# Low parts of every second weight block in two stages: from VectorE's subtraction to a transfer that adds in place

## The reference

```python
    y = h.astype(u.dtype) * jax.nn.silu(gate)
    return y @ w_out                                        # a_w_out
...
        h = h + _rmsnorm(y, norm_post[i])
        h = h + jax.nn.sigmoid(h @ ple_w_gate[i]) * (p[i] @ ple_w_proj[i])
```

## Time and profile before

| | |
|---|---|
| median of 3 runs | 2148.67 us (2148.39 to 2149.68) |
| span of the profiled execution | 2146.7 us; the median is 2.0 us above it |
| PE busy | 2101.1 us, 98% of the span |
| DVE busy | 1592.8 us, 74% |
| ACT busy | 1026.9 us, 48% |
| POOL busy | 99.5 us, 5% |
| DMA queue of SP | 445.78 MB, 61.1% of 16 engines |
| low parts by DVE | 636, 774.6 us |
| high parts by ACT | 636, 671.6 us |
| aout / the 12 single tiles of pleg | about 284.4 to 378.6 us / 428 to 496 us of the span |

### The profile page before, as it was taken

How to read it: one execution, slowest core, us unless ns; L and a number is a source line. 1 busy time by engine, 2 the same in 40 slices (tenths; PEclk the granted TensorE clock), 3 DMA queues, 4 the chain that set the end, 5 groups by cost and what they waited for, 6 DMA issues and landing times.

```text
span 2146.7 us, 31802 instructions
## 1 busy us (share of the span) xinstructions
PE 2101.1 (98%) x12800; PEld 1830.9 (85%) x12800; DVE 1592.8 (74%) x2357; ACT 1026.9 (48%) x1560; POOL 99.5 (5%) x81
## 2 busy tenths in 40 slices
PE   7999999999999999999999999999999999999997
PEld 7787799787888888899999888878888888888886
DVE  7778699698889777667877898576766766656655
ACT  5766344556532322555554455554444434434443
POOL 1000002020000000000000001210000000000012
PEclk9999999999999999999999999999999999999998
DMA  6556778676733567444346988645775765555552
GB/s 232 197 200 224 249 253 274 223 273 230 247 111 130 172 234 267 149 132 141 132 135 207 367 300 300 228 146 195 258 254 187 240 230 196 181 192 196 187 178 97
DMA packets 122402, 447.80 MB, mean 209 GB/s; under 512 B 13712, under 2 KB 13840, under 8 KB 121872
## 3 DMA queue, kind: packets, MB, share of 16 engines
q1 hardware_dynamic: 122256, 445.78, 61.1%
HBM read 441.53 MB, written 4.19 MB: 208 GB/s over the span
## 4 chain that ended last, share of the span: by engine, by line
PE 71%; DVE 2%; ACT 1%; issue 1%; POOL 0%; POOLq 0%; DVEq 0%; ACTq 0%
PE bank L826 70%; DVE WL L1499 0%; DVE AR L1506 0%; PE bank L955 0%; DVE SR L1506 0%; PE bank L986 0%; ACT WH L1093 0%; DVE AR L1499 0%; POOL AR L2102 0%; ACT AR L1094 0%; ACT AR L1093 0%; DVE AR L1599 0%; ACT SR L1094 0%; POOL AR L2104 0%; ACT L1094 0%
## 5 line engine op out<-in xcount | busy, mean ns | idle before, releaser
L826 PE MATMUL bank<-SR,WH 128*128 128x512 f32 (+1 forms) x6880 | 1811.5, 352 | 28.6 <-DVE WL L1499 10.7
L826 PE MATMUL bank<-SR,WL 128*128 128x256 f32 (+1 forms) x5088 | 1208.7, 288 | 0.5 <-DVE SR L1506 0.4
L826 PEld LDWEIGHTS bank<-SR,WH 128*128 128x128 f32 x6880 | 1096.0, 190 | 94.0 <-issue 30.6
L826 PEld LDWEIGHTS bank<-SR,WL 128*128 128x128 f32 x5088 | 963.7, 190 | 156.1 <-DVE SR L1506 1.9
L1499 DVE TENSOR_TENSOR WL<-WF,WH 128x1024 fp32r<-128x1024 f32 x636 | 774.6, 1229 | 221.2 <-ACT WH L1093 221.0
L1093 ACT ACTIVATE WH<-WF 128x1024 fp32r<-128x1024 f32 x636 | 671.6, 1057 | 463.4 <-PE bank L826 428.0
L1093 ACT ACTIVATE AR<-bank 128x256 f32<-128x256 f32 (+2 forms) x261 | 103.6, 407 | 277.8 <-PE bank L826 263.4
L1506 DVE SCALAR_TENSOR_TENSOR AR<-WF,SM,AR 128x512 f32<-128x512 f32 (+1 forms) x240 | 232.8, 1000 | 4.5
L1499 DVE TENSOR_TENSOR AR<-AR 128x256 f32<-128x256 f32 (+9 forms) x374 | 154.8, 445 | 58.4 <-ACT AR L1094 35.4
L2097 POOL TENSOR_TENSOR AR<-AR 128x256 f32<-128x256 f32 x56 | 74.2, 1325 | 2013.1 <-ACT AR L1094 2012.8
L1499 DVE TENSOR_TENSOR AR<-AR,bank 128x256 f32<-128x256 f32 x112 | 47.2, 421 | 119.2 <-PE bank L826 91.2
(11 more groups left out here) (75 smaller groups left out, 464.0 us busy)
## 6 DMA issues: line engine op xcount, KB each, us to landing
WF<-in_mlp SPq DMA_DIRECT2D x256, 512.0 KB, 4.2
WF<-in_mod SPq DMA_DIRECT2D x192, 512.0 KB, 4.9
WF<-in_w_in SPq DMA_DIRECT2D x176, 512.0 KB, 4.3
WF<-in_a_in SPq DMA_DIRECT2D x64, 512.0 KB, 4.7
WF<-in_a_out SPq DMA_DIRECT2D x32, 512.0 KB, 5.1
WF<-in_ple_g SPq DMA_DIRECT2D x32, 512.0 KB, 4.5
WF<-in_w_out SPq DMA_DIRECT2D x32, 512.0 KB, 5.6
WF<-in_pw SPq DMA_DIRECT2D x16, 512.0 KB, 3.2
```

What stands on the lines that cost most here:

```text
L826: return tensor.matmul(o, l, r, start=start, stop=stop, skip_group_check=True)
```

## The change

In the stages `aout` and `pleg` every second weight block (the second half of each tile, or every odd one of the eight) gets its low part in another way. Directly behind the rounded copy into `WH`, ACT writes a second copy with scale -1 into `WL` (semaphore `w_neg`). Then POOL issues a DMA that reads the same weight block from DRAM again and adds it onto `WL` where it lies (`accum_op=ALU.add`, one semaphore `w_add` for each `WL` buffer). The sum is the weight less its high part. DVE leaves these blocks out. They are 16 of the 32 blocks in each of the two stages, 32 of 636 in all. The load ring's buffer of such a block counts as free when the negated copy is made. POOL's program is now walked through the common list, so that its sums of squares and its DMAs stand in that order. The core of the diff:

```diff
+BY_DMA = ("a_out", "ple_g")
...
+        if b["of"] == "w":
+            b["by_dma"] = b["name"] in BY_DMA and whole % 2 == 1
+            b["kind"] = "d" if b["by_dma"] else "w"
+            whole += 1
...
     def freed(i):
         b = blocks[i]
-        return {"w": w_lo, "v": mod_v, "p": mod_p}[b["of"]], b["n"]
+        return {"w": w_lo, "d": w_neg, "v": mod_v, "p": mod_p}[b["kind"]], b["n"]
...
+    def low_ready(k):
+
+        if weights[k]["by_dma"]:
+            return w_add[k % NB], 16 * sum(b["by_dma"] for b in weights[k % NB:k + 1:NB])
+        return w_lo, weights[k]["n"]
...
             if part == "high":
                 w.wait_ge(w_hi, n + 1)
             else:
-                w.wait_ge(w_lo, n + 1)
+                w.wait_ge(*low_ready(n))
...
             act(WH[:, k % NB, :], WF[:, i % NF, :], ACT.Copy).then_inc(w_hi, 1)
+            if weights[k]["by_dma"]:
+                act(WL[:, k % NB, :], WF[:, i % NF, :], ACT.Copy, scale=-1.0).then_inc(w_neg, 1)
...
         def low_part(i, k):
+            if weights[k]["by_dma"]:
+                return
             w.wait_ge(w_hi, k + 1)
...
+        def low_part(k):
+            b = weights[k]
+            w.wait_ge(w_neg, b["n"])
+            pool.dma_start(WL[:, k % NB, :], ins[b["name"]][b["index"]][:, b["lo"]:b["lo"] + BLK],
+                           accum_op=ALU.add).then_inc(w_add[k % NB], 16)
...
+        def add_square(group, ft):
+            if 1 <= ft <= 14:
+                w.wait_ge(sq, 16 * group + ft + 1)
+                w.wait_ge(acc, 14 * group + ft - 1)
+                pool.tensor_tensor(ACC, ACC, SQ[ft % 2], ALU.add).then_inc(acc, 1)
...
+        for what, *a in steps:
+            if what == "low" and weights[a[1]]["by_dma"]:
+                low_part(a[1])
+            elif what == "evac":
```

More of the change, by code:

```diff
@@ L165, in timetable @@
     assert not mods and not spread
-    count = {"w": 0, "v": 0, "p": 0}
+    count = {"w": 0, "d": 0, "v": 0, "p": 0}
+    whole = 0
     for b in blocks:
-        count[b["of"]] += 1
-        b["n"] = count[b["of"]]
+        b["kind"] = b["of"]
+        if b["of"] == "w":
+            b["by_dma"] = b["name"] in BY_DMA and whole % 2 == 1
+            b["kind"] = "d" if b["by_dma"] else "w"
+            whole += 1
+        count[b["kind"]] += 1
+        b["n"] = count[b["kind"]]
     tile, uses = {}, [0] * 8
@@ L591, in build @@
     s_x = [sem(f"s_x{q}") for q in range(len(XPIECES))]
-    w_hi, w_lo, prod, mod_v, mod_p = (sem(n) for n in ("w_hi", "w_lo", "prod", "mod_v", "mod_p"))
+    w_hi, w_lo, w_neg, prod, mod_v, mod_p = (sem(n) for n in ("w_hi", "w_lo", "w_neg", "prod", "mod_v", "mod_p"))
+    w_add = [sem(f"w_add{i}") for i in range(NB)]
     free = [sem(f"free{g}") for g in range(GBANKS)]
@@ L741, in freed @@
         b = blocks[i]
-        return {"w": w_lo, "v": mod_v, "p": mod_p}[b["of"]], b["n"]
+        return {"w": w_lo, "d": w_neg, "v": mod_v, "p": mod_p}[b["kind"]], b["n"]
+    weights = [b for b in blocks if b["of"] == "w"]
+    def low_ready(k):
+        if weights[k]["by_dma"]:
+            return w_add[k % NB], 16 * sum(b["by_dma"] for b in weights[k % NB:k + 1:NB])
+        return w_lo, weights[k]["n"]
     def mod_blocks(cg):
@@ L2083, in pool_program @@
             pool.tensor_tensor(XPARTS[:, q, :], s[:, 0, :], s[:, 1, :], ALU.add).then_inc(x_part, 1)
[L2084 to L2089, removed]
+        def low_part(k):
[12 more added lines that the diff above has]
+            elif what == "evac":
+                kind, j = a[0]
+                if kind == "aout" or (kind == "wout" and a[0] in WHOLE):
+                    add_square(SQUARES[kind], j)
+                elif kind == "mlp2" and j[0] == 3:
+                    add_square(3, j[1])
+            elif what == "after" and (a[0], a[2]) == ("pleg", 3):
+                add_square(1, a[1])
+            elif what == "after" and (a[0], a[2]) == ("wout", 2) and (a[0], a[1]) not in WHOLE:
+                add_square(2, a[1])
+            elif what == "add_y2":
+                at, by = LAST[a[0]]
+                if by == "p":
+                    n = sum(b == "p" for _, b in LAST[:a[0]])
+                    w.wait_ge(st_rs, RECIP["y2"])
+                    w.wait_ge(*left(("wout", 15)))
+                    w.wait_ge(s_back, 16)
                     y = YO1[:, at:at + 2, :]
@@ L2093, in pool_program @@
                     pool.tensor_tensor(XT2[:, at:at + 2, :], XT2[:, at:at + 2, :], y, ALU.add).then_inc(x3_p, 1)
[L2094 to L2104, removed]
+            elif what == "finish":
+                w.wait_ge(y2_s, 1)
+                w.wait_ge(st_rs, RECIP["out"])
+                for n, at in enumerate(at for at, by in LAST if by == "p"):
+                    y = YO2[:, at:at + 2, :]
+                    pool.tensor_tensor(y, y, rs_b(RSTD[0], 2), ALU.mult).then_inc(p_own, 1)
+                    w.wait_ge(p_own, 7 + n + 1)
+                    pool.tensor_tensor(y, y, XT2[:, at:at + 2, :], ALU.add).then_inc(out_p, 1)
     blk = ctx.enter_context(nc.Block())
```

## The result

The changed kernel takes **2230.11 us** (median of 4 runs, 2228.96 to 2232.43) against 2149.18 us for the kernel before (4 runs, 2148.39 to 2150.12): ratio 1.0377, 95% interval 1.0362 to 1.0392. It is 81 us slower; 26 were predicted, and the value lies just above the range's upper end of 2230. The profiled execution has a span of 2227.9 us, 81.2 more than before.

The account below looks back on a forecast made before the run. PE was taken to bound the kernel. Late transfers cost 16 us in aout and 11 in pleg, DVE waits gave back 0.9: 2146.7 became 2172.8 us of span, plus 2.0 gives 2175 us; range 2148 to 2230.

Parts of the forecast that it names:

- What bounds the kernel: Whole kernel: PE bounds it; relieving DVE in aout and pleg can gain at most 0.9 us of PE's waits.
- The copies, SP, POOL's additions, all at zero: Both stages: ACT's 34 us of negated copies, SP's load issue and POOL's additions were each taken to cost nothing.
- The room: Time from the DMA's possible issue until PE needs the block: 5.6 us in aout, 5.1 us in pleg.
- the halving: Ring of four: every second block is late and gives time to the next, so a tile loses half the lateness.
- L: Time from w_neg to the semaphore of the transfer's last byte; taken as 7.4 us in aout, 6.8 in pleg.
- The prediction's own formula: If L exceeds the room, a tile loses (L - 5.6)/2 in aout and (L - 5.1)/2 in pleg.
- The size of L: Plain-load median 5.1 (aout) or 4.5 us (pleg), plus 1.3 second read, 1.0 POOL issue: 7.4 and 6.8 us.
- the sum: Whole kernel: 16 us lost in aout, 11 in pleg, 0.9 gained from DVE waits; span 2172.8 us.
- The check by bytes: In aout 2.62 MB a tile at 396 GB/s takes 6.6 us, taken to agree with the latency sum.
- the latency sum: In aout a tile takes 5.76 + (7.4 - 5.6)/2 = 6.66 us.
- Hidden: Rival, 18%: transfers land within 5.1 us of issue, PE never waits, about 2148 us.
- Much slower: Rival, 20%: adding transfer far below plain rate or POOL issue slow beside DVE; 2209 (L 9.5) to 2259 us (L 13.0).

Follow-up runs that it names:

- the scratch version: Against the kernel before: ACT writes 30 of the 32 negated copies into two buffers nobody reads, no transfers, DVE makes every low part; 2148.39 us, ratio 1.0.
- high products first: Against the changed kernel: in treated blocks PE takes all products with the high part, then waits for the transfer and takes the low ones; 2183.91 us.
- the traffic alone: Against the changed kernel: adding transfers go into two buffers nobody reads, DVE makes every low part, no negated copies on ACT; 2159.54 us, ratio 1.0053.
- the added products: Against the kernel treating aout alone (2193.79 us): 16 useless PE products ahead of each treated block, 256 in all, 31 us of work; 2190.53 us.

## Why the prediction was right in sign and wrong in size

**What bounds the kernel: right.** Taking 38 us off DVE bought nothing; PE's wait on DVE inside the stages was 0.9 us, and that is gone.

**The copies, SP, POOL's additions, all at zero: right.** The copies by the scratch version (ratio 1.0). Between 283 and 590 us PE waits for nothing but the two kinds of transfer. POOL's issue takes 0.89 us in the row above; 1.0 was taken.

**The room (5.6 and 5.1 us) and the halving: right.** With the measured landing, and 0.3 us from `w_neg` to the issue (316.24 to 316.54), L is 9.3 us in aout and 9.4 in pleg. The prediction's own formula then gives 16 x (9.3 - 5.6)/2 = 30 us, measured 31.3, and 12 x (9.4 - 5.1)/2 = 26 us, measured 25.9. With high products first it gives 16 x (9.3 - 7.5)/2 = 14, measured 13.5; with plain transfers (L = 7.3) 14, measured 13.9. For every fourth block in aout it is less close: with that kernel's own landing (L = 9.8) 8 x 4.2 = 34, measured 30.9. Only the pattern was misjudged: the text said one wait of 0.9 us to a tile, where its own formula has one wait to two tiles. In aout there are nine waits, seven of them of 3.1 to 5.0 us.

**The size of L: the step that failed.** The prediction added up 7.4 us in aout and 6.8 in pleg, "from the median of the plain loads at the same places, 5.1 us in aout and 4.5 us in pleg", 1.3 us for the second read and 1.0 us for the issue on POOL. Measured were 9.3 and 9.4. The run without the addition divides the miss. In aout 0.3 us from `w_neg` to the issue had no term; the plain transfer by POOL landed in 7.0 where 5.1 + 1.0 was taken, 0.9 more; and the addition put 2.0 on that where 1.3 was taken, 0.7 more: 1.9 in all. In pleg, where the plain transfers landed in 6.2, it is 0.3, 0.7 and 1.6: 2.6 in all. Every term was short, in pleg the addition's most. The division is as good as the comparison of two kernels that also differ in their waits.

Nor does L follow the landing of the plain loads, from which it was estimated. In aout the adding transfers landed in 9.5 us where the plain loads took 5.2 (every fourth block), in 9.0 where they took 7.8 (the changed kernel), and in 8.8 where they took 11.1 (the traffic alone). In the sum, 27 us of waits for transfers were expected (16 and 11) and 57.2 came.

**PE's clock: the term that was missing.** The sum priced a wait at its length. But the waits of 3 to 5 us cost the clock too (0.89 in aout, 0.95 in the window of pleg), and PE's busy time rose by 26.5 us. Eight stretches of aout and five of pleg stand at a clock of 0.50 or 0.51 (one of them, and the sums of aout's and of pleg's, with PE's busy time):

```profile
363.40:366.80 3.40, 3.40 (x18) 0.50 1.06 272
sum 30.60, PE 27.86; mean PE 3.48
...
sum 17.00, PE 16.67; mean PE 3.33
```

If products started there every 0.21 us instead of every 0.12, the stretches cost 12 us in aout and 7 in pleg, an estimate from these rows. In aout the added products bear it out: they gave back 10 us of the 13. For pleg no such run was made, and 6 of the 13 us of busy time there stay unexplained.

So: 30 us from L and 26.5 us from PE's busy time on top of the 26 predicted; shorter waits elsewhere give back 1.6 of these, which leaves the 81.2 measured.

**The check by bytes: near as a floor, wrong as support.** It said 6.6 us a tile. The kernel with traffic alone has 15 tiles from 290.93 to 386.43, 6.4 us each, at a DMA share of 1.00, and the one with high products first 6.8 at 1.01. That this agreed with 6.66 from the latency sum said nothing of L: a floor by bytes bounds the beat from below only, and the changed kernel stands at 8.5 with the engines at 0.86 over the stage.

**The rivals.** *Hidden* would have needed a landing within 5.1 us. Those of pleg's transfers in the kernel after:

```profile
DMA to landing us min/median/max: 6.1/9.1/11.9
```

Not even the fastest did it. The rule of the Trainium skill, page "DMA: Bandwidth & Descriptors", section "Anatomy of one DMA — SWDGE (gpsimd) path", would give an estimate of 3.2 us. Under this load a plain transfer issued by POOL took 7.0 in aout and an adding one 9.0.

*Much slower* is the case whose times (2209 to 2259) hold the result, though L stayed just below its bound of 9.5 and the clock made up the rest. So the number falls there, but only in part by that rival's mechanism. Of its two reasons the rate of the addition is right (1.78), the slow issue beside DVE is not: the issues took 0.86 to 1.01 us. The Trainium skill, page "SBUF — State Buffer", section "Who interferes with whom", says that its own probe showed no stall of a DMA beside `tensor_tensor`. The low parts on DVE are of that kind, so these runs do not test the page's warning. In the kernel with every fourth block the transfer issued at 317.44 moved no packet for 5.1 us either, and DVE was busy for only 1.7 of them.

**What stays open.** What an adding packet does in its 1.78-fold time, and what holds a transfer's first packet back for about 5 us, as in the example from 316.54: no run had a transfer without plain loads beside it. Nor did any version of the change come below the kernel before.

## What to carry to other kernels

A helper that is nearly full but in time is worth nothing to relieve, and the path that relieves it must fit the ring: set the room (buffers ahead times the beat, less what precedes the issue) against a measured landing of the new kind of transfer under its own traffic, not against the landing of other loads. Price a wait of several microseconds on TensorE with the slower products behind it, here about half as much again. And look at what an experiment's own scaffolding waits for: two of the first four had a wait of their own that was as large as what they measured.

## What the runs showed of the hardware that had not been expected

- A transfer that adds in place held a DMA engine about 1.78 times as long a packet as the same transfer without the addition (1426 against 802 us for 4608 packets), and landed in 9.0 us instead of 7.0.
- The landing of adding transfers in aout stayed at 8.8 to 9.5 us while that of the plain loads beside them went from 5.2 (8 such transfers) over 7.8 (16) to 11.1 (16 that nobody waits for).
- A transfer of POOL can stand for half of its landing time without one packet moving, 4.9 of 9.6 us in the example, at a DMA share of 0.74.
- A 4.02 us wait of PE was followed by products 0.21 us apart instead of 0.12, for 3 us.
- Work of no use on PE, 31 us of it, did not make the kernel slower, since it filled waits and kept the clock.
